# Hybrid mixer block: decay sums one level earlier, window-attention scores from stacked split operands, gate slices last in a step

## The reference, cut to what matters

```python
# B: q (8 heads of 64), k and v (2 heads of 64); blocks of 128 queries see the block before, their own and the next
s_loc = where(valid, einsum('bhgnqd,bhnkd->bhgnqk', qb, kb) * scale, NEG_INF)   # |i - j| <= 128
s_ctx = einsum('bhgnqd,bhcd->bhgnqc', qb, kc) * scale                           # 256 context keys
pr = softmax(concatenate([s_ctx, s_loc, s_sink]))
o = einsum('bhgnqc,bhcd->bhgnqd', pr[..., :256], vc) + einsum('bhgnqk,bhnkd->bhgnqd', pr[..., 256:640], vb)

# C: S_t = diag(a_t) S_{t-1} + k_t^T v_t,  o_t = q_t S_t, 4 heads with 64 key and 128 value channels, both directions
la_f = log_sigmoid(lr_f @ w_decay[0] + b_decay[0]) / 16
y = rmsnorm(o_f + flip(o_b), norm_w) * silu(gate)

z = einsum('blnw,nwd->blnd', stack(ys), w_branch)
x = x + mod[2] * (einsum('blnd,blnd->bld', sigmoid(gate_logits), z) @ w_o)
```

## Time and profile before

| | |
|---|---|
| median of 3 runs | 3343.31 us (3334.99 to 3349.95) |
| the profiled execution | 3357.3 us |
| its span | 3355.6 us |
| TensorE products busy | 3134.9 us, 93%, 16256 instructions |
| VectorE busy | 1414.6 us, 42% |
| ScalarE busy | 1167.2 us, 35% |
| mean granted TensorE clock | 0.964 |

### The profile page before, as it was taken

How to read it: one execution, slowest core, us unless ns; L and a number is a source line. 1 busy time by engine, 2 the same in 40 slices (tenths; PEclk the granted TensorE clock), 3 DMA queues, 4 the chain that set the end, 5 groups by cost and what they waited for, 6 DMA issues and landing times.

```text
span 3355.6 us, 39886 instructions
## 1 busy us (share of the span) xinstructions
PE 3134.9 (93%) x16256; PEld 2418.2 (72%) x16256; DVE 1414.6 (42%) x2288; ACT 1167.2 (35%) x2019; POOL 165.6 (5%) x179
## 2 busy tenths in 40 slices
PE   6988899999999999899999989888999999889998
PEld 4877785577667768788888867777456567578887
DVE  4266742333443435423232332774333444454444
ACT  4343333333443343412121234443332443442222
POOL 0023300000000000000000000320000000000000
PEclk8999998999999999999999989999997999999999
DMA  5222240031103123233333322223021021323332
GB/s 186 75 84 79 81 135 25 19 106 62 52 27 113 59 92 102 78 105 101 101 106 102 95 82 60 85 76 126 7 80 47 13 89 48 107 76 100 94 99 90
DMA packets 83759, 273.82 MB, mean 82 GB/s; under 512 B 9344, under 2 KB 9600, under 8 KB 82688
## 3 DMA queue, kind: packets, MB, share of 16 engines
q1 hardware_dynamic: 74896, 229.84, 21.7%
q0 software_dynamic: 8688, 41.49, 3.7%
HBM read 245.07 MB, written 26.21 MB: 81 GB/s over the span
## 4 chain that ended last, share of the span: by engine, by line
PE 87%; ACT 5%; DVE 5%; issue 2%; DMA 2%; SPq 0%; DVEq 0%; ACTq 0%
PE slot L615 84%; PE slot L1019 2%; DMA raw<-w_merge_dram 1%; ACT tmp L1209 1%; DVE wl L1517 1%; ACT PT_B L1392 0%; ACT Hh L1211 0%; DMA SS<-g_kept 0%; ACT wh L1118 0%; DVE XS L1783 0%; ACT Yh L1386 0%; ACT logits_out L1161 0%; DVE XS L1722 0%; DMA X<-xT_dram 0%; DMA g_kept<-logits_out 0%
## 5 line engine op out<-in xcount | busy, mean ns | idle before, releaser
L615 PE MATMUL slot<-Hh,wh 128*128 128x512 f32 (+1 forms) x2368 | 885.9, 375 | 48.4 <-DVE Hl L1564 15.1
L615 PE MATMUL slot<-Hl,wh 128*128 128x512 f32 (+1 forms) x2368 | 843.2, 357 | 0.0
L615 PE MATMUL slot<-Hh,wl 128*128 128x512 f32 (+1 forms) x2368 | 841.9, 357 | 0.0
L615 PEld LDWEIGHTS slot<-Hh,wh 128*128 128x128 f32 x2368 | 455.4, 193 | 166.4 <-issue 77.7
L615 PEld LDWEIGHTS slot<-Hh,wl 128*128 128x128 f32 x2368 | 455.2, 193 | 64.9
L615 PEld LDWEIGHTS slot<-Hl,wh 128*128 128x128 f32 x2368 | 456.3, 193 | 61.1 <-issue 5.8
L1517 DVE TENSOR_TENSOR wl<-raw,wh 128x1024 fp32r<-128x1024 f32 (+1 forms) x208 | 228.5, 1099 | 232.5 <-ACT wh L1118 229.5
L1841 DVE TENSOR_REDUCE rowmax<-slot 128x1 f32<-128x768 f32 (+3 forms) x160 | 123.4, 771 | 412.6 <-PE slot L615 412.0
L615 PE MATMUL slot<-Uh,wh 128*128 128x512 f32 (+1 forms) x768 | 274.3, 357 | 0.0
L615 PE MATMUL slot<-Ul,wh 128*128 128x512 f32 (+1 forms) x768 | 272.0, 354 | 0.0
L615 PE MATMUL slot<-Uh,wl 128*128 128x512 f32 (+1 forms) x768 | 271.5, 354 | 0.0
(11 more groups left out here) (229 smaller groups left out, 4099.8 us busy)
## 6 DMA issues: line engine op xcount, KB each, us to landing
raw<-w_dram SPq DMA_DIRECT2D x204, 512.0 KB, 3.6
raw<-w_gate_dram SPq DMA_DIRECT2D x64, 512.0 KB, 3.6
ada_g_raw<-ada_dram POOLq DMA_DIRECT2D x48, 512.0 KB, 3.9
ada_g_raw<-ada_dram SPq DMA_DIRECT2D x32, 512.0 KB, 3.9
raw<-w_merge_dram SPq DMA_DIRECT2D x64, 256.0 KB, 2.7
g_kept<-logits_out SPq DMA_DIRECT2D x32, 384.0 KB, 2.3
SS<-g_kept SPq DMA_DIRECT2D x32, 384.0 KB, 3.3
ada_first<-ada_dram SPq DMA_DIRECT2D x8, 1024.0 KB, 18.2
```

The source lines that it names most:

```text
L615: return pe.matmul(dst, lhsT, rhs, start=start, stop=stop)
```

## The change

**B.** k is projected first. After the rotary step each q row is split: its high part goes to the head's own 64 partitions of `QS`, its low part to the other 64. k's high part is put in both halves of `K_HIGH`, its low part in both halves of `K_LOW`. One product of 128 channels with `K_HIGH` and one with `K_LOW` give all four partial scores, over all near blocks at once. The masks are split-type too, from copies in the place of the rotary tables. Attention waits for `split_low` and `masks_split`.

**C.** `decay_logits` of the next head come ahead of level 6 instead of level 7, and `decay_sums` ahead of the last overlay. ScalarE makes the inter-chunk factors before the norm factors and the whole gates' copies, and level 0's exponentials before these copies as well. TensorE waits for one whole gate's copy at level 0 and for the other at level 1. In layer 1 a slice comes after the level's product instead of before.

**A, B and D.** The slice comes last in a step, after the transposes.

```diff
     "A": [("cq", 0), ("cq", 1), ("ckv", 0)],
-    "B": [("q", j) for j in range(4)] + [("k", 0), ("v", 0)],
+    "B": [("k", 0)] + [("q", j) for j in range(4)] + [("v", 0)],
...
-        QB, KB = XS[:, 1:5, :], XS[:, 0, :]
+        QS = rows("QS", R_X, B_HEADS, f32r)
+        KS = [rows(f"KS{k}", R_S + k, 1, f32r) for k in range(3)] + [rows("KS3", R_S + 12, 1, f32r)]
+        K_HIGH, K_LOW = [KS[0][:, 0, :], KS[1][:, 0, :]], [KS[2][:, 0, :], KS[3][:, 0, :]]
+        QT = [SS[:, 3 + k, :] for k in range(3)]
         KD = at("KD", [2, T], f32, (R_X + 4) * ROW)
-        VT = {"C": [XS[:, 4, :], XS[:, 5, :]], "B": [XS[:, 6, :], XS[:, 6, :]], "D": [XS[:, 6, :], XS[:, 7, :]]}
-        VB = at("VB", [NB, P], f32, (R_X + 5) * ROW)
+        VT = {"C": [XS[:, 4, :], XS[:, 5, :]], "B": [SS[:, 6, :], SS[:, 6, :]], "D": [XS[:, 6, :], XS[:, 7, :]]}
+        VB = at("VB", [NB, P], f32, (R_S + 11) * ROW)
...
-                return QB[:, j, :] if kind == "q" else KB
+                return QT[(1 + j if kind == "q" else 0) % 3]
...
                     for n in range(len(LEVELS) + 1):
-                        if n == len(LEVELS) and h + 1 < C_HEADS:
+                        if n == len(LEVELS) - 1 and h + 1 < C_HEADS:
                             decay_logits(h + 1)
...
                         more = steps[h * (len(LEVELS) + 1) + n]
-                        if nq == SEQ:
-                            for step in more:
-                                later_gate(layer, level_gate(layer, h, step[0]), *step[1:])
-                        if n == 0:
-                            pe.wait_ge(logits_copied.sem, parts_done[0])
+                        if n < 2:
+                            pe.wait_ge(logits_copied.sem, parts_done[0] - (WHOLE_GATES[layer] - 1 if n == 0 else 0))
                         pe.wait_ge(*slots.next(("level", where), acc_first if n == 0 else lvl_read))
                         if n != 1:
...
                                 last = mm(level_ctx_at[where][:, d], left[:, s], right[:, s])
                         last.then_inc(lvl_done.sem, 1)
+                        if nq == SEQ:
+                            for step in more:
+                                later_gate(layer, level_gate(layer, h, step[0]), *step[1:])
                         if n == 0:
...
                         if branch == "B":
                             g, j = tile["g"], tile["j"]
-                            part = slice(g * B_HD, (g + 1) * B_HD)
-                            q = QB[part, j, qs_]
-                            for x, m in enumerate(tile["keys"][:tile["lat"]]):
-                                dst = out_s[:, a + x * P:a + (x + 1) * P]
-                                edge = m != n
-                                mm(dst, q, KB[part, m * P:(m + 1) * P], start=True, stop=not edge)
-                                if edge:
-                                    mm(dst, ident[:, :], winmask[:, 0 if m < n else 1, :], start=False, stop=True)
-                            last = mm(out_s[:, SEQ:T], q, KB[part, SEQ:T])
+                            q = QS[:, 2 * j + g, qs_]
+                            near = tile["keys"][:tile["lat"]]
+                            edges = [m for m in near if m != n]
+                            if near:
+                                keys = slice(near[0] * P, (near[-1] + 1) * P)
+                                mm(out_s[:, a:SEQ], q, K_HIGH[g][:, keys], start=True, stop=False)
+                                mm(out_s[:, a:SEQ], q, K_LOW[g][:, keys], start=False, stop=False)
+                            for m in edges:
+                                dst = out_s[:, a + (m - near[0]) * P:a + (m - near[0] + 1) * P]
+                                mm(dst, ident_r[:, :], winmask_r[:, 0 if m < n else 1, :], start=False, stop=m == edges[-1])
+                            mm(out_s[:, SEQ:T], q, K_HIGH[g][:, SEQ:T], start=True, stop=False)
+                            last = mm(out_s[:, SEQ:T], q, K_LOW[g][:, SEQ:T], start=False, stop=True)
...
                                 else:
                                     last = mm(out_s[:, lo:hi], QY[:, h, qs_], KD[:, h // (D_HEADS // D_KV), lo:hi])
                         last.then_inc(scores_done.sem, 1)
-                        for step in steps[i]:
-                            later_gate(layer, FIRST_GATE[layer][branch] + step[0], *step[1:])
                     if i > LAG and tiles[i - LAG - 1]["last"]:
...
                             units += 1
                             values_in += 1
+                    if i < len(tiles):
+                        for step in steps[i]:
+                            later_gate(layer, FIRST_GATE[layer][branch] + step[0], *step[1:])
                 chain_over(("c0", "c1", ("unit", 0), ("unit", 1), "values"))
...
                         branch_a(nq)
-                    if b == "B" and layer == 0:
-                        pe.wait_ge(masks_in.sem, w.next(masks_in, 2))
+                    if b == "B":
+                        pe.wait_ge(split_low.sem, w.next(split_low, B_SPLITS))
+                        pe.wait_ge(masks_split.sem, w.next(masks_split))
...
-                        act.activation(QB[:, j, 0:nn] if kind == "q" else KB[:, 0:nn], s[:, 0:nn], ACT.Copy).then_inc(copied.sem, 1)
+                        if n >= 3:
+                            act.wait_ge(split_low.sem, w.next(split_low))
+                        act.activation(rotated("B", kind, j)[:, 0:nn], s[:, 0:nn], ACT.Copy).then_inc(copied.sem, 1)
...
+                def split_into_high(kind, j):
+
+                    act.wait_ge(roped.sem, w.next(roped))
+                    src = rotated("B", kind, j)
+                    for g in range(B_KV):
+                        part = slice(g * B_HD, (g + 1) * B_HD)
+                        if kind == "q":
+                            ins = act.activation(QS[part, 2 * j + g, 0:nq], src[part, 0:nq], ACT.Copy)
+                        else:
+                            for copy in range(2):
+                                ins = act.activation(K_HIGH[g][copy * B_HD:(copy + 1) * B_HD, 0:T], src[part, 0:T], ACT.Copy)
+                    ins.then_inc(split_high.sem, 1)
+
+                if branch == "B":
+                    act.wait_ge(roped.sem, w.next(roped, 4 + (6 if layer else 0)))
...
+                    if branch == "B" and n >= 2 and plan[n - 2][0] in "qk":
+                        split_into_high(*plan[n - 2])
...
+                if branch == "B":
+                    if layer == 0:
+                        act.wait_ge(masks_in.sem, w.next(masks_in, 2))
+                    act.activation(ident_r[:, :], ident, ACT.Copy)
+                    act.activation(winmask_r[:, :, :], winmask[:, :, :], ACT.Copy).then_inc(masks_split.sem, 1)
+                    act.wait_ge(split_low.sem, w.next(split_low, B_SPLITS - 2))
...
                 def levels_over():
 
-                    act.wait_ge(lvl_done.sem, w.next(lvl_done, len(LEVELS)))
                     act.wait_ge(q_ready.sem, w.next(q_ready, 2))
                     act.wait_ge(k_ready.sem, w.next(k_ready, 2))
 
                 for h in range(C_HEADS):
                     if h > 0:
-                        norm_factors()
                         levels_over()
 
-                    for i in range(WHOLE_GATES[layer] - 1):
-                        whole_out(layer, i, True)
                     act.wait_ge(diff_ready.sem, w.next(diff_ready))
                     act.activation(ee[0][f, 0:T], cumy[f, 0:T], ACT.Exp, scale=1.0 / C_TEMP)
                     act.activation(ee[0][b, 0:T], diff[0][b, 0:T], ACT.Exp, scale=1.0 / C_TEMP)
@@ -1323,8 +1360,8 @@
                     act.activation(ee[1][b, 0:T], cumy[b, 0:T], ACT.Exp, scale=1.0 / C_TEMP)
                     act.activation(dec[:, :], tot[:, :], ACT.Exp, scale=1.0 / C_TEMP).then_inc(inter_e.sem, 1)
                     if h > 0:
-                        output_high(h - 1)
-                    whole_out(layer, WHOLE_GATES[layer] - 1, True)
+                        norm_factors()
+                        act.wait_ge(lvl_done.sem, w.next(lvl_done, len(LEVELS)))
                     for n, m in enumerate(LEVELS):
                         if n == 0:
 
@@ -1340,8 +1377,13 @@
                         act.activation(e[:, :, 0:m], d[:, :, 0:m], ACT.Exp, scale=-1.0 / C_TEMP)
                         act.activation(e[:, :, m:2 * m], d[:, :, m:2 * m], ACT.Exp, scale=1.0 / C_TEMP).then_inc(e_ready.sem, 1)
                         if n == 0:
+                            if h > 0:
+                                output_high(h - 1)
+                            whole_out(layer, 0, True)
                             act.wait_ge(kt_done.sem, w.next(kt_done))
                             act.activation(kit, slot[0][:, 0:T], ACT.Copy).then_inc(kt_copied.sem, 1)
+                            for i in range(1, WHOLE_GATES[layer]):
+                                whole_out(layer, i, True)
                         if n == 1:
```

(41 more changed lines are left out.)

11 lines of the change are left out of this document (9 added, 2 removed).

## The result

The changed kernel takes 3246.41 us (median of 4 runs, 3240.14 to 3253.28) where the kernel before takes 3339.15 beside it (4 runs, 3328.05 to 3349.95). The ratio is 0.9723, with a 95% interval from 0.9686 to 0.9759: 93 us won. The prediction was 3270, range 3240 to 3308. The profiled execution went from 3357.3 to 3240.1 us, so the sum, made against the profile, promised 87 and the profile shows 117.

A forecast was written before the change was run, and what follows sets the result against it. TensorE, with 87% of the chain, was taken to bound the kernel. From the profiled 3357.3 us: - 79 (B's scores) - 18 + 6 (clock) + 12 (B's projection) - 8 (C) = 3270, range 3240 to 3308.

The forecast's parts named there:

- B's scores, -79: Branch B's attention, both layers: fewer, split-type score products shorten TensorE's work; 79 us gained after waits on other engines.
- The bound at TensorE alone, 97: Branch B's scores: 97 us gained if TensorE never waits for the other engines.
- Slices last, 0: Steps of A, B and D: putting the slice last moves no work; zero gain, bounds 5 us either way.
- The clock spell, -18 +6: Layer 1's B: split-type products bring the clock back, 18 us gained; two short spells at B's starts cost 6.
- (1): Rival in B: other engines take over, no step under 3 us; 30 us more, 3300; chance 0.17 together with (2).
- (2): Rival in B's scores: short masks run like single-precision ones; 31 us more, 3301; chance 0.17 together with (1).
- (3): Rival in C: decays through early, each head change loses its 5.07 us idle; 17 to 20 more won, 3252; chance 0.12.
- (4): Rival in B: attention stays at the lower clock, up to 140 and 100 us more, about 3500; chance 0.06.
- The starts, +12: B's projection and attention starts, both layers: splits on ScalarE and VectorE delay them; 12 us lost, bounds 6 and 16.
- C, -8: Branch C, layer 0: first head gains 7 us, three head changes 0.5 each, layer 1 nothing; 8 us gained.

The follow-up runs named there:

- B's part alone: The kernel before with only B's projection, splits and new scores, C's order and slices as before: 3249.91 us against 3345.76, ratio 0.972.
- the pair with slices first and last: The changed kernel with the slice put back ahead of the transposes, 3246.95 us, and the changed kernel itself, 3246.41 us, on other chips.
- Slices last alone: The kernel before with only the slice moved behind the transposes in A, B and D: 3316.13 us, ratio 0.991.
- The padded kernel: The changed kernel with B's scores in single precision, q zero-padded to 128 partitions, one product over all near blocks, single-precision masks: 3269.38 us, ratio 0.9801.
- the version with both moved back: The changed kernel with decay_sums back behind the last overlay and norm_factors back ahead of the inter-chunk factors: 3219.27 us, ratio 0.9649.

## Why the prediction was right, and where it was off

The forecast held: B's scores decide, and the time fell in the range. Without the clock its sum was -79 + 12 - 8 = -75, and the timed runs have -81; for the clock it had -12, and they have -11. That the clock agrees so closely is in part luck, as the spell in layer 1 was 48 us in one profile of the kernel before and 34 in the other. Term by term:

- **B's scores, -79.** Right, shown by the kernel with B's part alone. The price of a tile was 0.78 and is 0.84; 0.58 is 0.58. The short mask, for which no row stood, was taken at 0.10; a lone one is followed after 0.06 (780.21 to 780.27 in the trace). From the first tile to D's rotation, layer 0 won 48 us (45). In layer 1, B's stage won 47.9; 18.2 of it is clock, and the start lost some 7 (1.7 of it clock), so its steps won about 35 (34). The bound at TensorE alone, 97, was not reached for the reason given: waits for `PT_B`, up to 2 us, and steps with a median of 2.6 us in layer 1, as predicted. They came to 29.3 us in all, 21.5 more than before, where I had counted 18 in waits of all kinds.

The Trainium skill, TensorE: Matmul & The Clock Gate, section Back-to-back issue gap, has some 81 ns for a product of 128 columns among weight loads; the trace has 60 for a split-type one in that place. The measurement decides; over the 96 masks the difference would be 2 us, an estimate from the page's figure.

- **Slices last, 0.** Wrong by itself: 30 us in the old kernel. The step that failed is "It moves no work", from which I concluded that it moves no wait either. In the old kernel the waits for logits copies were 17.3 us, in a row of the list of waits that I left out of the sum; 6 of them go. The larger part is clock: 20 us in the timed runs, and in the profile that of layer 1's B. In the changed kernel, though, the slices' place is worth 0 to 4 us, and rather against the change (the pair with slices first and last), so for this change the 0 was nearly right by luck: there, what the copies of logits give, the copies of probabilities take.
- **The clock spell, -18 +6.** Near in size: 23.9 us lost in layer 1's B before, 5.7 after, and 1.7 more in layer 0's stage, together -16.5 where the sum had -12; My reason, the split-type products, is not shown. Slices last alone also kept the clock, in its one profile. The padded kernel, whose scores are single-precision, was back at the full clock by 2514, some 7 us behind layer 1's first tile at 2507.27 (0.59 from 2506 to 2514, behind 4.08 us of idle). And layer 0 came back after some 10 us with the old scores. With the new scores the spell was short in every profile; what does it stays open. The clock is also why the parts don't add up. B's part won 96 us, C's order 17, slices last 30, together 143, and the whole 93. What both B's part and the slices' place show in their profiles is the removal of the clock spell in layer 1, which can be removed only once; the timed runs agree, with 45 us of clock won by the parts and 11 by the whole. The waits for ScalarE's copies are also common to both.
- **The rivals.** (1) came in part: the waits for `PT_B` are there, but only three of 24 steps in layer 1 take over 3 us. (2) fell; even with single-precision masks the kernel is only some 4 us slower, not 31. (3) gave 3252, nearer to the median of 3246 than the forecast, but its mechanism isn't there: the idle at each change of head was moved, not lost; the version with both moved back, without most of it, is at 3219. (4) fell: B ran at 0.98 and 1.00. The Trainium skill, same page, Part 4, says that transposes don't count as busy time in the way that products do. These runs hardly test it: transposes took 11% of layer 0's attention before and after, and 12% of layer 1's, so they did not grow to a quarter of the time as I had counted for a step.
- **The starts, +12.** The wait was worked out as 6.9 us behind v's job and is 7.1; the idle 5.16 and 4.10. Up to B's first tile layer 0 takes 3.5 us more and layer 1 7.1, together 10.6, and the first slice comes later besides. Right.
- **C, -8.** The walk through VectorE's queue gave an idle of 5.5 ahead of the output; 5.38 stands there. From head 0's level 0 to head 2's level 0 it takes 134.66 us (181.83 to 316.49) instead of 135.31 (187.81 to 323.12): 0.65 over two changes of head, where I said 0.5 for each. The first head won 7.6 (7). Of these 7.6, 3.4 are clock. Alone in the old kernel C's order won 17 by the medians and 14 by the means of the table, 10.5 of it clock; beside the new scores it won 3. What I didn't do with this walk is ask what the other order would give: the sums ahead of the overlay, with the norm factors moved to suit them, are the wrong half of the change and cost 27 us, which the version with both moved back regains.
- **The 30 us by which the profile beat the sum** are some 19 of clock (31 in all where the sum had 12; 14 of them outside the stages with B, most in C, A and the long stage between, up to 4 us each) and about 11 of small gains, 3 of them in B in layer 0, 1 in layer 1. I didn't trace each. The medians show 93, near the 87 of the sum: part of the 30 is that the profiled execution of before was a long one.

**Open.** Why the clock falls behind 1.3 or 1.41 us of idle in some profiles and not in others, why it then comes back after some 10 us in layer 0 and after 34 to 48 in layer 1, and how the slices' place bears on it. Layer 0's slices are on the whole longer (six products of 512 columns behind the tile of the earlier trace rows; some in layer 1 have three); no run changes their length. The timed runs tell how much of a gain is clock, but not at which place in the kernel.

## What to carry to other kernels

Here small products on half the partitions paid more for their shape than for their type: try stacking operands so that a product fills the 128 partitions and covers all its blocks, and measure the type apart from it. Before you move a chain ahead in an engine's queue, list what the busiest engine needs from behind it: five us of sums ahead of an overlay were five us of idle TensorE, six times. And when an edit moves no work, still look at the list of waits, for it may change who is waited for; test it in the kernel with the other edits: alone the slices' place was worth 30 us, there next to nothing. And split every timed difference by the granted clock before you explain it: 20 of those 30 us were clock.
